# Forgetting attention: queries turned by VectorE in 32x32 blocks instead of by TensorE, and the order of the work around it

## The chip, the core and the metric

The kernel runs on one core of a Trainium2 chip. The metric is the device time of one execution in microseconds (us). Each engine has an instruction queue of its own, worked off in order; engines wait for each other only by counting semaphores. The short names of the profile are used below: PE is TensorE (PEld its weight loads), DVE is VectorE, ACT is ScalarE, POOL is GpSimd, SP issues the weight DMAs.

## The reference, cut to what matters

Two transformer blocks are computed for 256 tokens of width 1024, in fp32. The change is in the first block, which has three mixers side by side (memory cross attention, gated linear attention, forgetting attention). The forgetting attention, with 4 heads of width 128, is:

```python
def _fox(q, k, v, log_f):
    scale = hd ** -0.5
    cum = jnp.cumsum(log_f, axis=-1)
    ...
        logits = (jnp.einsum('bhqd,bhkd->bhqk', q_i, k) * scale
                  + c_i[..., None] - cum[:, :, None, :])
        p = jax.nn.softmax(jnp.where(mask, logits, -jnp.inf), axis=-1)
        return jnp.einsum('bhqk,bhkd->bhqd', p.astype(v.dtype), v)

o_fox = _fox(_rmsnorm(_heads(fq, 4), g_fox_q), _rmsnorm(_heads(fk, 4), g_fox_k), _heads(fv, 4), log_f)
gates = jax.nn.sigmoid(bg + b_gate)      # merged = sum over mixers of gates * (y_b @ w_branch[b])
```

The gains `g_fox_q` and `g_fox_k` belong to the 128 columns of a head, so the product q.k only sees their product, column by column.

## The kernel before, in words

**Weights.** All weights come as 186 granules, nearly all of 128 x 2048 fp32 (1 MB), through a ring of four slots. Per granule, ACT makes the high part (`Wh`, line 1273), DVE the low part (`Wl = raw - Wh`, line 1810), and PE multiplies three times (high x high, low x high, high x low; line 689). A granule is 24 matmuls of 512 columns, 12 for each of the two tiles of 128 tokens. ACT may write a slot of `Wh` when PE has done the granule four earlier (`gran_used`); DVE follows ACT (`hi_ready`); PE and the next DMA follow DVE (`lo_ready`).

**The order of the work** is written by hand, engine by engine. A weight unit is 512 output columns; on ACT and DVE `unit(name, read_out, *urgent)` splits the first granule of the unit four places on, then does the given steps, then splits the last one. The units around the change stand in this order on PE: fq, fk, fv, gate_mem0, gate_gla0, gate_fox0, branch_mem0, branch_gla0, branch_fox0, gate_mem1. A gate unit has two granules, a branch unit one. Each unit's product lies in two of four PSUM banks `ps`, so a unit may start only when the unit two places earlier has been read out of its banks (`drained`). For the gate units DVE takes the product out (line 2027), ACT works on it in the same bank (abs, exp, ln; lines 1480 to 1482), and DVE takes that out (line 2037). For branch_mem0 DVE multiplies out of the bank into `merged` (line 2049).

**The small work** goes through four other PSUM banks `aux0` to `aux3`; `plan_aux` lists which use has which bank, and a use may start when the one before it was read (`aux_free`). Transposes of rows (tokens on partitions) to columns (`turn_rows`, line 761) are PE matmuls with an identity: four blocks of 128x128 for one bank. Then ACT or DVE copy the bank to SBUF. In the forgetting attention: POOL norms the rows `FQ` and `FK`; PE turns `FQ` into banks 0 and 1 and `FK` into banks 2 and 3; ACT copies the first two to `fqT` with the query gain (line 1497), DVE the other two to `fkT` with the key gain (line 1901). One unit later PE makes the scores (`fsc`, lines 1014 and 1015), head h in bank h. DVE adds the forget terms and takes the maximum (lines 2085 to 2093), ACT makes exponentials (line 1452), DVE norms them (`normed`, line 2011), PE turns them (`fpT`, line 761), ACT and DVE copy them, and PE attends (`foT`, line 977). ACT and DVE make high and low parts of the result, `yTh_fox` and `yTl_fox` (line 1829), the operands of branch_fox0.

**What stands around it.** The memory attention's result `moT` takes bank h for head h just ahead of the turns of `FQ` and `FK`; its low parts `yTl_mem` (line 1829) free these banks. The gated linear attention's result `GG` is turned into banks 0 and 1 (`gyT`) between the two granules of gate_gla0; ACT makes `yTh_gla` (line 1304) and DVE `yTl_gla` (line 1834), which frees these two banks for the scores of heads 0 and 1. On ACT and DVE the splits of the second granule of gate_fox0 and of branch_mem0 stand ahead of these two.

Of the kernel before, what the change touches and what calls it, by code (L numbers as in the profile page):

```python
# [22 lines left out]
ALU = mybir.AluOpType  # L23
ACT = mybir.ActivationFunctionType
AX = mybir.AxisListType

P = 128
TOK = 256
# [9 lines left out]
HD = 128  # L38
# [98 lines left out]
def plan_aux():  # L137

    plan, used = {}, [0] * 4

    def use(name, banks, first=0):
        for b, bank in enumerate(banks):
            used[bank] += 1
            plan[(name, first + b)] = (bank, used[bank])

    use("memT", [0, 1, 2, 3])
    use("xT", [0, 1, 2, 3])
    use("small", [0])
    use("rows20", [1])
    use("gaT", [1])  # L150
    use("z", [0])
    use("mkT", [2, 3])
    use("foxcum", [1])
    use("cum", [2])
    use("suf", [3])
    use("dec", [0])
    use("mqT", [1, 2])
    use("foxT", [0])
    use("gqT", [3])
    use("gkT", [0])  # L160
    use("attn", [1, 2])
    use("cs", [3, 0])
    use("o", [1, 2])
    use("msc", [0, 1, 2, 3])
    use("mpT", [0, 1, 2, 3])
    use("moT", [0, 1, 2, 3])
    use("fqT", [0, 1])
    use("fkT", [2, 3])
    use("gyT", [0, 1])
    use("fsc", [0, 1, 2, 3])  # L170
    use("fpT", [0, 1, 2, 3])
    use("foT", [0, 1, 2, 3])
    use("mgT", [0, 1, 2, 3])
    use("x1T", [0, 1, 2, 3])
    use("ffT10", [0])
    use("x2T", [0, 1, 2, 3])
    use("rsc", [0, 1, 2, 3])
    for h in range(4):
        use(f"ro{h}", [2 * h % 4, 2 * h % 4 + 1])
    for h in range(4):  # L180
        use(f"ryT{h}", [2 * h % 4, 2 * h % 4 + 1])
    use("x3T", [0, 1, 2, 3])
    use("x4T", [0, 1, 2, 3])
    use("bqT0", [0, 1])
    use("bkT0", [2, 3])
    use("bsc", [0, 1, 2, 3])
    use("bqT1", [0, 1])
    use("bkT1", [2, 3])
    use("bpT", [0, 1, 2, 3])
    use("bsc", [0, 1, 2, 3], 4)  # L190
    use("boT", [0, 1, 2, 3])
    use("bpT", [0, 1, 2, 3], 4)
    use("boT", [0, 1, 2, 3], 4)
    use("x5T", [0, 1, 2, 3])
    return plan
# [89 lines left out]
def build(nc, wstream, x_in, mem_in, cpack, gpack, wsmall, w_a2, b_a, b_fox, b_gate, post, rett, mobat, dmask, out):  # L285
    ctx = ExitStack()
    with ctx:
# [4 lines left out]
        def at(name, shape, kb, dt=F32):  # L292
            return nc.alloc_sbuf_tensor_at(name, shape, dt, offset=BASE + int(kb * KB))
# [11 lines left out]
        R = 131  # L305
# [12 lines left out]
        FQ = at("FQ", [P, 2, C], R + 24)  # L318
# [15 lines left out]
        mqT = at("mqT", [P, 4, TOK], R + 52)  # L334
        mkT = at("mkT", [P, 4, TOK], R + 56)
        fpT = at("fpT", [P, 4, 2, TOK], R + 52)
        fqT = at("fqT", [P, 4, TOK], R + 60)
        fkT = at("fkT", [P, 4, TOK], R + 64)
        mpT = at("mpT", [P, 4, 2, TOK], R + 60)
        gqT = at("gqT", [P, 2, TOK], R + 60)  # L340
# [2 lines left out]
        prob = at("prob", [P, 4, 2, TOK], R + 68)  # L343
# [63 lines left out]
        def gcol(name, k=0):  # L407
            o, _ = GAIN_COLS[name]
            return gains[:, o + k:o + k + 1]

        def S(name, a=0, b=None):
            o, w = SCAL[name]
            return sc[:, o + a:o + (w if b is None else b)]
# [16 lines left out]
        def sem(name):  # L430
            if name not in sems:
                sems[name] = ctx.enter_context(nc.semaphore(name))
            return sems[name]
# [43 lines left out]
        def wait_aux(eng, name, b=0):  # L477
            k, n = AUX[(name, b)]
            eng.wait_ge(aux_ready[k], n)
            return aux[k]  # L480
# [6 lines left out]
        def free(ins, name, b=0):  # L487

            return ins.then_inc(aux_free[AUX[(name, b)][0]], 1)
# [191 lines left out]
        def _(pe):  # L681
# [82 lines left out]
            def turn_rows(name, rows, b):  # L764

                turn(name, b, [(kk * TOK + t * P, rows[:, t, (2 * b + kk) * P:(2 * b + kk + 1) * P])
                               for kk in range(2) for t in range(2)])
# [21 lines left out]
            def wait_operand(name, banks):  # L789

                for b in banks:
                    wait_read(pe, name, b)
# [55 lines left out]
            o = open_aux("rows20")  # L848
# [14 lines left out]
            o = open_aux("z")  # L863
# [17 lines left out]
            for name, mat in (("cum", "chunk_upto"), ("suf", "chunk_after")):  # L881
                o = open_aux(name)
# [3 lines left out]
            o = open_aux("dec")  # L886
# [34 lines left out]
            for b, chunks in enumerate(((0, 2), (1,))):  # L921
                o = open_aux("cs", b)
# [69 lines left out]
            for h in range(4):  # L992
                wait_read(pe, "mpT", h)
                attend("moT", h, lambda ks: MV[:, ks, h * HD:(h + 1) * HD], mpT)
            pe.wait_ge(sem("fq_unit"), 1)
            for b in range(2):
                turn_rows("fqT", FQ, b)
            pe.wait_ge(sem("fk_unit"), 1)
            for b in range(2):
                turn_rows("fkT", FK, b)  # L1000
# [6 lines left out]
            product("gate_gla0", (xTh, xTl), before={1: turn_gla})  # L1007

            wait_operand("fqT", range(2))  # L1010
            wait_operand("fkT", range(2))
            for h in range(4):
                o = open_aux("fsc", h)
# [231 lines left out]
        def _(act):  # L1245
# [29 lines left out]
            def unit(name, read_out=None, *urgent):  # L1275

                for g in range(G[name], GEND[name] - 1):
                    split(g + RING)
                if read_out:  # L1280
                    read_out()
                for step in urgent:
                    step()
                split(GEND[name] - 1 + RING)
# [188 lines left out]
            def gate_log(b, n, tiles=(0, 1)):  # L1473
                def go():

                    k = 3 * n + BRANCHES.index(b)
                    for t in tiles:
                        o = bank(f"gate_{b}{n}", t)
                        act.wait_ge(sem("gate_z"), 2 * k + t + 1)
                        link(nc.scalar.activation(o, gate[b][:, t, :], ACT.Abs))  # L1480
                        link(nc.scalar.activation(o, o, ACT.Exp, scale=-1.0))
                        nc.scalar.activation(o, o, ACT.Ln, bias=1.0).then_inc(sem("gate_log"), 1)
                return go
# [6 lines left out]
                for h in range(4):  # L1490
                    high("moT", h, yT["mem"][0], (h,))

            def fq_turned():
                act.wait_ge(sem("q_gains"), 2)
                for b in range(2):
                    o = wait_aux(act, "fqT", b)
                    free(nc.scalar.activation(fqT[:, 2 * b:2 * b + 2, :], o[:, :], ACT.Copy, scale=S("gfq_s")), "fqT", b)

            def mem_probs():
                for h in (0, 2):  # L1500
                    probs_T("mpT", h, mpT)

            unit("gate_mem0", mem_probs, mem_high, gate_log("mem", 0), fq_turned)

            def gla_high():
                for b in range(2):
# [290 lines left out]
        def _(dve):  # L1797
# [15 lines left out]
            def unit(name, read_out=None, *urgent):  # L1813
                for g in range(G[name], GEND[name] - 1):
                    split(g + RING)
                if read_out:
                    read_out()
                for step in urgent:
                    step()
                split(GEND[name] - 1 + RING)  # L1820
# [75 lines left out]
            def turned(name, b, dst, scale=None):  # L1896
                o = wait_aux(dve, name, b)
                if scale is None:
                    free(nc.vector.tensor_copy(dst, o[:, :]), name, b)
                else:  # L1900
                    free(nc.vector.tensor_scalar(dst, o[:, :], scale, None, ALU.mult), name, b)
# [25 lines left out]
                low("xT", b, xTl, xTh, (2 * b, 2 * b + 1), "g_mix")  # L1927
            split(3)
            nc.vector.tensor_scalar(S("gmq_s"), gcol("g_mq"), float(HD) ** -0.5, None, ALU.mult).then_inc(sem("q_gains"), 1)
            nc.vector.tensor_scalar(S("gfq_s"), gcol("g_fq"), float(HD) ** -0.5, None, ALU.mult).then_inc(sem("q_gains"), 1)  # L1930
            x_stats("x0")
            unit("mk")
            head_sums("mk")
# [72 lines left out]
            def normed(k, h, pr, rec, total, widths):  # L2006

                link(nc.vector.reciprocal(rec(0, 2), total(0, 2)))
                for t in range(2):
                    v = pr[:, h % 4, t, 0:widths[t]]  # L2010
                    nc.vector.tensor_scalar(v, v, rec(t, t + 1), None, ALU.mult).then_inc(sem(f"{k}_prob"), 1)  # L2011
# [3 lines left out]
                normed("m", h, prob, lambda a, b: S("ms_rec", 2 * h + a, 2 * h + b),  # L2015
                       lambda a, b: S("ms_sum", 2 * h + a, 2 * h + b), (TOK, TOK))
            head_sums("fk")
            unit("fv")

            def gate_rows(b, n):  # L2020

# [12 lines left out]
            def gate_lsig(b, n, t):  # L2034

                dve.wait_ge(sem("gate_log"), 2 * (3 * n + BRANCHES.index(b)) + t + 1)
                nc.vector.scalar_tensor_tensor(out=gate[b][:, t, :], in0=gate[b][:, t, :], scalar=0.0,
                                               in1=bank(f"gate_{b}{n}", t), op0=ALU.min,
                                               op1=ALU.subtract).then_inc(drained["dve"], 1)
# [21 lines left out]
                for h in range(4):  # L2061
                    low("moT", h, yT["mem"][1], yT["mem"][0], (h,))

            def fk_turned():
                for b in range(2):
                    turned("fkT", b, fkT[:, 2 * b:2 * b + 2, :], gcol("g_fk"))

            def mem_probs():
                for h in (1, 3):
                    turned("mpT", h, mpT[:, h, :, :])  # L2070
                gate_rows("mem", 0)()

            unit("gate_mem0", mem_probs, mem_low, lambda: gate_lsig("mem", 0, 0), lambda: gate_lsig("mem", 0, 1), fk_turned)

            def gla_low():
                for b in range(2):
# [16 lines left out]
                    nc.vector.tensor_reduce(S("fs_nm", 2 * h + 1, 2 * h + 2), prob[:, h, 1, :], AX.X, ALU.max, negate=True)\  # L2093
                        .then_inc(sem("f_max"), 1)

            unit("gate_gla0", gla_low, fox_scores)
            for h in range(4):
                dve.wait_ge(sem("f_exp"), 2 * h + 2)
                normed("f", h, prob, lambda a, b: S("fs_rec", 2 * h + a, 2 * h + b),
                       lambda a, b: S("fs_sum", 2 * h + a, 2 * h + b), (P, TOK))  # L2100
            def fox_probs():
                for h in (1, 3):
                    o = wait_aux(dve, "fpT", h)
# [436 lines left out]
```

## Time and profile before

| | |
|---|---|
| median of 3 runs | 1113.65 us (1113.42 to 1113.72) |
| the profiled execution's own time | 1113.15 us |
| its span in the profile | 1111.4 us |
| granted TensorE clock | 1.00 of full speed |
| PE busy | 1102.1 us, 99% of the span |
| DVE, ACT, POOL busy | 70%, 57%, 14% |
| the changed stretch | about 132 to 190 us of the span |

Times in the rows are from the start of the span. In a timeline row stand the start, the length from the first start to the last end, engine, line, operation, output<-input, sizes and count; an idle time ahead of it and who ended it stand in square brackets. Consecutive instructions of an engine overlap by a little, so starts are further apart than the idle time alone would say, and closer than the durations.

### The profile page before, as it was taken

The page shows a single profiled execution, that of the slowest core. Times are in us where ns is not written, and L with a number is a line of the kernel's source. Part 1 is how long each engine was busy: PE and PEld are TensorE (multiplying, and loading weights), DVE is VectorE, ACT ScalarE, POOL GpSimd, SP SyncE. Part 2 cuts the span into 40 slices and gives each one's busy share as a digit, 9 for nine tenths or more (in the row PEclk, how much of TensorE's full clock was granted, in tenths as well). Part 3 has the DMA queues.
Part 4 walks back from the last instruction along what each step waited for, and adds up shares of the span by engine and source line. Part 5 has one row for each costly group of instructions (what it writes and reads, how often), then busy time and mean ns, then how long its engine had stood idle before and what let it go on. Part 6 is the DMA issues. An engine that isn't in the chain of part 4 may idle for free.

```text
span 1111.4 us, 13482 instructions
## 1 busy us (share of the span) xinstructions
PE 1102.1 (99%) x5152; PEld 916.3 (82%) x5152; DVE 781.5 (70%) x858; ACT 636.8 (57%) x788; POOL 153.3 (14%) x111
## 2 busy tenths in 40 slices
PE   8999999999999999999999999999999999999997
PEld 7788888888888888888888888888888888888886
DVE  5745668776568883678448569998465776899942
ACT  6655566655767653654587366554355545656431
POOL 1433700000343410000023000000016100000000
PEclk9999999999999999999999999999999999999999
DMA  9645344645555555555535456546555334545530
GB/s 355 237 169 180 118 185 144 226 171 193 178 197 207 186 185 197 219 208 192 187 114 195 165 184 252 190 156 230 197 186 199 124 139 171 215 173 185 191 145 38
DMA packets 30503, 205.17 MB, mean 185 GB/s; under 512 B 3624, under 2 KB 3792, under 8 KB 6768
## 3 DMA queue, kind: packets, MB, share of 16 engines
q1 hardware_dynamic: 28752, 198.75, 49.4%
q0 software_dynamic: 1696, 5.64, 1.6%
q8 instruction: 39, 0.64, 0.2%
q14 instruction: 16, 0.13, 0.0%
HBM read 203.33 MB, written 1.05 MB: 184 GB/s over the span
## 4 chain that ended last, share of the span: by engine, by line
PE 94%; DVE 3%; ACT 1%; issue 1%; DMA 1%; SPq 0%; DVEq 0%; ACTq 0%
PE ps L689 83%; PE ps L1108 3%; PE aux L761 3%; PE ps L1110 1%; PE ps L811 1%; PE aux L977 1%; PE aux L1145 1%; DMA mrows<-in_mem 1%; ACT Wh L1273 1%; PE aux L1132 0%; DVE sc L2425 0%; DVE Wl L1810 0%; PE aux L963 0%; DVE bprob L2440 0%; DVE prob L2011 0%
## 5 line engine op out<-in xcount | busy, mean ns | idle before, releaser
L689 PE MATMUL ps<-Wh,xT 128*128 128x512 f32 x1792 | 561.3, 391 | 0.0
L1810 DVE TENSOR_TENSOR Wl<-raw,Wh 128x2048 fp32r<-128x2048 f32 x184 | 425.1, 2318 | 181.8 <-ACT Wh L1273 180.9
L1273 ACT ACTIVATE Wh<-raw 128x2048 fp32r<-128x2048 f32 x184 | 350.9, 1914 | 191.2 <-PE ps L689 190.3
L689 PEld LDWEIGHTS ps<-Wh,xT 128*128 128x128 f32 x1792 | 336.5, 188 | 69.9 <-issue 0.7
L689 PE MATMUL ps<-Wl,xT 128*128 128x512 f32 x896 | 348.8, 389 | 0.0
L689 PEld LDWEIGHTS ps<-Wl,xT 128*128 128x128 f32 x896 | 168.3, 188 | 34.3
L689 PE MATMUL ps<-Wh,hTh 128*128 128x512 f32 x256 | 99.8, 390 | 0.0
L689 PE MATMUL ps<-Wh,hTl 128*128 128x512 f32 x256 | 99.7, 389 | 0.0
L689 PE MATMUL ps<-Wl,hTh 128*128 128x512 f32 x256 | 99.7, 389 | 0.0
L2353 DVE STREAM_TRANSPOSE htmp<-held 32x512 f32<-32x512 f32 x128 | 89.9, 703 | 2.7
L641 POOL TENSOR_TENSOR sc<-sc,cst 128x1 f32<-128x1 f32 x8 | 4.5, 558 | 443.0 <-DVE sc L2313 443.0
L689 PEld LDWEIGHTS ps<-Wh,hTh 128*128 128x128 f32 x256 | 48.1, 188 | 10.0
L689 PEld LDWEIGHTS ps<-Wl,hTh 128*128 128x128 f32 x256 | 48.1, 188 | 9.9
L689 PEld LDWEIGHTS ps<-Wh,hTl 128*128 128x128 f32 x256 | 48.1, 188 | 9.9
L1108 PE MATMUL ps<-xT,Wh 128*128 128x512 f32 x128 | 45.3, 399 | 0.0
L525 POOL TENSOR_TENSOR sc<-sc,cst 128x8 f32<-128x8 f32 (+1 forms) x11 | 17.9, 1631 | 166.9 <-DVE sc L1877 146.1
L1698 ACT ACTIVATE held<-ps 128x512 f32<-128x512 f32 x32 | 18.8, 595 | 32.8 <-PE ps L689 32.8
L1110 PE MATMUL ps<-xT,Wl 128*128 128x256 f32 x128 | 36.0, 281 | 0.0
L689 PE MATMUL ps<-Wh,ffTh 128*128 128x512 f32 x88 | 34.4, 391 | 0.0
L689 PE MATMUL ps<-Wh,ffTl 128*128 128x512 f32 x88 | 34.3, 390 | 0.0
L689 PE MATMUL ps<-Wl,ffTh 128*128 128x512 f32 x88 | 34.3, 389 | 0.0
L1317 ACT ACTIVATE xT<-aux,gains 128x128 fp32r<-128x128 f32 x80 | 21.7, 383 | 21.6 <-PE aux L761 21.6
(354 smaller groups left out, 1296.5 us busy)
## 6 DMA issues: line engine op xcount, KB each, us to landing
raw<-in_wstream SPq DMA_DIRECT2D x185, 1024.0 KB, 4.8
grow<-in_post_gains POOLq DMA_DIRECT2D x4, 512.0 KB, 5.6
grow<-in_b_gate POOLq DMA_DIRECT2D x6, 256.0 KB, 3.5
mrows<-in_mem SPq DMA_DIRECT2D x2, 512.0 KB, 5.2
raw<-in_wstream SPq DMA_DIRECT2D x2, 512.0 KB, 6.4
x<-in_x SPq DMA_DIRECT2D x1, 1024.0 KB, 14.6
out<-x SPq DMA_DIRECT2D x4, 256.0 KB, 2.0
rdm<-in_ret_decays POOLq DMA_DIRECT2D x1, 768.0 KB, 5.1
```

Source lines behind the costliest of these rows:

```text
L525: nc.gpsimd.tensor_tensor(S(f"{key}_rstd", 0, n), S(f"{key}_var", 0, n), K("minus_half").broadcast_to([P, n]), ALU.pow).then_inc(sem("norm ...
L689: mm = nc.tensor.matmul(ps[2 * pair + t][:, :], a[:, kt, t * P:(t + 1) * P], w[:, slot, j, :], start=(first and j == 0 and q == 0), stop=( ...
L761: tr = nc.tensor.transpose(o[0:src.shape[1], at:at + P], src, ident)
L811: mm = nc.tensor.matmul(bank("mk", t), a[:, 4 * g + j, t * P:(t + 1) * P], w[:, g, j, :], start=(g == 0 and j == 0 and q == 0), stop=(g == ...
L977: mm = nc.tensor.matmul(o[:, q0:TOK], v(ks), pT[:, h % 4, ks, q0:TOK], start=(ks == 0), stop=(ks == 1))
L1108: nc.tensor.matmul(o[:, :], Wh[:, g % RING, kt % 4, w], xT[:, kt, :, :], start=(kt == 0), stop=False, skip_group_check=True)
L1110: mm = nc.tensor.matmul(o[:, 0:TOK], Wl[:, g % RING, kt % 4, w], xTh[:, kt, :], start=False, stop=(kt == DK - 1), skip_group_check=True)
L1273: nc.scalar.activation(split_view(Wh, g), weight_view(raw, g), ACT.Copy).then_inc(hi_ready, 1)
L1317: nc.scalar.activation(dst[:, k0 + j, t * P:(t + 1) * P], o[:, j * P:(j + 1) * P], ACT.Copy, scale=gcol(gain, k0 + j)).then_inc(sem(f"{nam ...
L1698: nc.scalar.activation(held[:, n // 2, t, n % 2, :], bank(name, t), ACT.Relu).then_inc(drained["act"], 1)
L1810: nc.vector.tensor_tensor(split_view(Wl, g), weight_view(raw, g), split_view(Wh, g).bitcast(F32), ALU.subtract).then_inc(lo_ready, 1)
L2353: i = nc.vector.transpose(dst[b:b + 32, :, :, a:a + 32], src[a:a + 32, :, :, b:b + 32])
```

## The change

1. PE no longer turns `FQ` (8 transposes of 128x128 gone); banks 0 and 1 lose one use. DVE turns it itself, SBUF to SBUF, by 16 transposes of 32x32 blocks, each over both token tiles and four heads (32 partitions x 256 elements). Eight stand inside unit fv, between its two splits, and eight at the end of gate_mem0, ahead of its last split.
2. `fkT` is copied by ACT, without a gain, in place of the two copies of `fqT`. The key gain is multiplied into the query gain `gfq_s`. When DVE has turned the queries (`fq_turned`), ACT scales all of `fqT` in place by it, one instruction of 128x1024. Only then does ACT go on to its next split. PE's scores wait for this (`fq_scaled`).
3. `fqT` lies at another place in SBUF, where `mkT` was.
4. The norming of the forgetting attention's probabilities moves ahead of the last split of gate_gla0 on DVE.

```diff
-    use("fqT", [0, 1])
...
-        fqT = at("fqT", [P, 4, TOK], R + 60)
+        fqT = at("fqT", [P, 4, TOK], R + 56)
...
-            pe.wait_ge(sem("fq_unit"), 1)
-            for b in range(2):
-                turn_rows("fqT", FQ, b)
...
-            wait_operand("fqT", range(2))
+            pe.wait_ge(sem("fq_scaled"), 1)
...
-            def fq_turned():
+            def fox_turned():
+                for b in range(2):
+                    o = wait_aux(act, "fkT", b)
+                    free(nc.scalar.activation(fkT[:, 2 * b:2 * b + 2, :], o[:, :], ACT.Copy), "fkT", b)
                 act.wait_ge(sem("q_gains"), 2)
-                for b in range(2):
-                    o = wait_aux(act, "fqT", b)
-                    free(nc.scalar.activation(fqT[:, 2 * b:2 * b + 2, :], o[:, :], ACT.Copy, scale=S("gfq_s")), "fqT", b)
+                act.wait_ge(sem("fq_turned"), 1)
+                nc.scalar.activation(fqT[:, :, :], fqT[:, :, :], ACT.Copy, scale=S("gfq_s")).then_inc(sem("fq_scaled"), 1)
...
-            nc.vector.tensor_scalar(S("gfq_s"), gcol("g_fq"), float(HD) ** -0.5, None, ALU.mult).then_inc(sem("q_gains"), 1)
+            nc.vector.scalar_tensor_tensor(out=S("gfq_s"), in0=gcol("g_fq"), scalar=float(HD) ** -0.5, in1=gcol("g_fk"),
+                                           op0=ALU.mult, op1=ALU.mult).then_inc(sem("q_gains"), 1)
...
-            unit("fv")
+
+            def turn_heads(key, rows, dst, first, last):
+
+                dve.wait_ge(sem(f"{key}_unit"), 1)
+                src = rows[:, :, :].rearrange("p t (h d) -> p t h d", d=HD)
+                cols = dst[:, :, :].rearrange("p h (t j) -> p t h j", j=P)
+                for ab in range(first, last):
+                    a, b = 32 * (ab // 4), 32 * (ab % 4)
+                    i = nc.vector.transpose(cols[b:b + 32, :, :, a:a + 32], src[a:a + 32, :, :, b:b + 32])
+                if last == 16:
+                    i.then_inc(sem(f"{key}_turned"), 1)
+
+            unit("fv", lambda: turn_heads("fq", FQ, fqT, 0, 8))
...
-            unit("gate_mem0", mem_probs, mem_low, lambda: gate_lsig("mem", 0, 0), lambda: gate_lsig("mem", 0, 1), fk_turned)
+            unit("gate_mem0", mem_probs, mem_low, lambda: gate_lsig("mem", 0, 0), lambda: gate_lsig("mem", 0, 1),
+                 lambda: turn_heads("fq", FQ, fqT, 8, 16))
...
-            unit("gate_gla0", gla_low, fox_scores)
-            for h in range(4):
-                dve.wait_ge(sem("f_exp"), 2 * h + 2)
-                normed("f", h, prob, ...)
+            unit("gate_gla0", gla_low, fox_scores, fox_normed)
```

Where it moves instructions on DVE, at the end of gate_mem0 and the start of gate_gla0. Before:

```order
L1829 TENSOR_TENSOR yTl_mem<-aux,yTh_mem 128x256 x4
L2037 SCALAR_TENSOR_TENSOR gate_mem<-gate_mem,ps 128x512 x2
L1901 TENSOR_SCALAR fkT<-aux,gains 128x512 x2
L1810 TENSOR_TENSOR Wl<-raw,Wh 128x2048 x2
L1834 SCALAR_TENSOR_TENSOR yTl_gla<-aux,gains,yTh_gla 128x256 x4
```

The same place of the changed kernel, whose line numbers differ by a few:

```order
L1827 TENSOR_TENSOR yTl_mem<-aux,yTh_mem 128x256 x4
L2048 SCALAR_TENSOR_TENSOR gate_mem<-gate_mem,ps 128x512 x2
L2025 STREAM_TRANSPOSE fqT<-FQ 32x2x4x32 x8
L1808 TENSOR_TENSOR Wl<-raw,Wh 128x2048 x2
L1832 SCALAR_TENSOR_TENSOR yTl_gla<-aux,gains,yTh_gla 128x256 x4
```

Eight transposes stand where two copies stood, ahead of two splits and of the instructions that free the banks of `gyT`.

On ACT, at the same place. Before:

```order
L1482 ACTIVATE ps<-ps 128x512
L1497 ACTIVATE fqT<-aux,sc 128x512 x2
L1273 ACTIVATE Wh<-raw 128x2048 x2
L1304 ACTIVATE yTh_gla<-aux,gains 128x256 x4
```

And in the changed kernel:

```order
L1478 ACTIVATE ps<-ps 128x512
L1492 ACTIVATE fkT<-aux 128x512 x2
L1495 ACTIVATE fqT<-fqT,sc 128x1024
L1269 ACTIVATE Wh<-raw 128x2048 x2
L1300 ACTIVATE yTh_gla<-aux,gains 128x256 x4
```

One instruction is new, and it waits for DVE's transposes; the two splits stand behind it.

## Rows read from the trace of the kernel before

**Rows 1.** The page's busy time, share of the span and instructions

```profile
PE 1102.1 (99%) x5152; PEld 916.3 (82%) x5152; DVE 781.5 (70%) x858; ACT 636.8 (57%) x788; POOL 153.3 (14%) x111
```

**Rows 2.** Waits of PE's weight loads, whole span: total, times, longest us

```profile
PEld ps L797 <- DVE warm L1914: 1.5, 1, 1.5
PEld aux L761 <- DVE prob L2011: 0.3, 1, 0.3
```

**Rows 3.** The chain of waits in this stretch: start, length, what

```profile
154.42 1.93 ACT Wh L1273
...
175.29 0.55 PE aux L761 x3
```

**Rows 4.** Timeline of PE

```profile
146.92 1.04 PE L761 MATMUL aux<-cst,FQ 128*128 128x128 f32 x8
...
148.58 0.47 PE L689 MATMUL ps<-Wh,xT 128*128 128x512 f32 x1
...
160.49 0.38 PE L1014 MATMUL aux<-fkT,fqT 128*128 128x128 f32 x2
...
161.14 0.38 PE L1014 MATMUL aux<-fkT,fqT 128*128 128x128 f32 x2
...
162.92 0.58 PE L689 MATMUL ps<-Wh,xT 128*128 128x512 f32 x1
...
174.00 1.84 PE L761 MATMUL aux<-cst,prob 128*128 128x128 f32 x12
...
189.23 0.39 PE L689 MATMUL ps<-Wh,yTh_fox 128*128 128x512 f32 x1
```

**Rows 5.** Timeline of DVE

```profile
147.53 0.42 DVE L1829 TENSOR_TENSOR yTl_mem<-aux,yTh_mem 128x256 fp32r<-128x256 f32 x1 [0.44 <-ACT yTh_mem L1300]
...
151.59 1.40 DVE L1901 TENSOR_SCALAR fkT<-aux,gains 128x512 f32<-128x512 f32 x2
153.97 4.70 DVE L1810 TENSOR_TENSOR Wl<-raw,Wh 128x2048 fp32r<-128x2048 f32 x2 [0.97 <-ACT Wh L1273]
158.58 1.66 DVE L1834 SCALAR_TENSOR_TENSOR yTl_gla<-aux,gains,yTh_gla 128x256 fp32r<-128x256 f32 x4
...
170.32 2.28 DVE L1810 TENSOR_TENSOR Wl<-raw,Wh 128x2048 fp32r<-128x2048 f32 x1
...
174.69 0.55 DVE L2011 TENSOR_SCALAR prob<-prob,sc 128x128 f32<-128x128 f32 x2
...
188.14 1.41 DVE L2049 TENSOR_TENSOR merged<-ps,gate_mem 128x512 f32<-128x512 f32 x2
```

**Rows 6.** Waits of DVE between 130 and 149 us

```profile
DVE Wl L1810 <- ACT Wh L1273: 2.0, 1, 2.0
DVE yTl_mem L1829 <- ACT yTh_mem L1300: 1.8, 4, 0.5
DVE gate_mem L2027 <- PE ps L689: 1.1, 1, 1.1
```

**Rows 7.** Timeline of ACT

```profile
152.01 1.93 ACT L1273 ACTIVATE Wh<-raw 128x2048 fp32r<-128x2048 f32 x1
154.42 1.92 ACT L1273 ACTIVATE Wh<-raw 128x2048 fp32r<-128x2048 f32 x1 [0.48 <-PE ps L689]
...
184.47 1.05 ACT L1487 ACTIVATE gate_fox<-gate_fox 128x1024 f32<-128x1024 f32 x1
185.42 1.19 ACT L1300 ACTIVATE yTh_fox<-aux 128x256 fp32r<-128x256 f32 x4
```

**Rows 8.** DVE transposes of 32x256 in the feed-forward stage, timeline

```profile
396.96 3.12 DVE L2154 STREAM_TRANSPOSE ftmp<-fpair 32x256 f32<-32x256 f32 x7
```

**Rows 9.** Timeline of PE at the start of the span

```profile
1.51 3.85 PE L797 MATMUL ps<-warm 128*128 128x512 f32 x9 [1.51 <-DVE warm L1914]
...
6.61 1.64 PE L797 MATMUL ps<-warm 128*128 128x512 f32 x6
9.18 1.09 PE L761 MATMUL aux<-cst,mrows 128*128 128x128 f32 x8 [0.93 <-DMA mrows<-in_mem]
```

More of the change, by code:

```diff
@@ L1501, in mem_probs @@
                     probs_T("mpT", h, mpT)
-            unit("gate_mem0", mem_probs, mem_high, gate_log("mem", 0), fq_turned)
+            unit("gate_mem0", mem_probs, mem_high, gate_log("mem", 0), fox_turned)
             def gla_high():
@@ L2062, in mem_low @@
                     low("moT", h, yT["mem"][1], yT["mem"][0], (h,))
-            def fk_turned():
-                for b in range(2):
-                    turned("fkT", b, fkT[:, 2 * b:2 * b + 2, :], gcol("g_fk"))
             def mem_probs():
@@ L2094, in fox_scores, with fox_normed @@
                         .then_inc(sem("f_max"), 1)
-            unit("gate_gla0", gla_low, fox_scores)
-            for h in range(4):
-                dve.wait_ge(sem("f_exp"), 2 * h + 2)
-                normed("f", h, prob, lambda a, b: S("fs_rec", 2 * h + a, 2 * h + b),
-                       lambda a, b: S("fs_sum", 2 * h + a, 2 * h + b), (P, TOK))
+            def fox_normed():
+                for h in range(4):
+                    dve.wait_ge(sem("f_exp"), 2 * h + 2)
+                    normed("f", h, prob, lambda a, b: S("fs_rec", 2 * h + a, 2 * h + b),
+                           lambda a, b: S("fs_sum", 2 * h + a, 2 * h + b), (P, TOK))
+            unit("gate_gla0", gla_low, fox_scores, fox_normed)
             def fox_probs():
```

## The prediction, made before the changed kernel was run

> **What bounds the kernel now.** I read the page's busy times first: PE works 1102.1 of 1111.4 us, the others have room [rows 1]. So work taken from PE is worth its time, and work given to another engine costs nothing as long as PE never waits for it. PE's waits come next: after the start there is one of 0.3 us for the norming of probabilities at DVE [rows 2]. The chain of waits says how near PE is to more of them: from 154.42 us on it leaves PE, runs through ACT's and DVE's splits and comes back to PE at 175.29, at the turn of these probabilities [rows 3]. In this stretch DVE and ACT have no time to give away. The timelines then give the distance between PE and each thing it waits for. One measure is used throughout: DVE's norming ended at 174.69 + 0.55 = 175.24 [rows 5] and PE went on at 175.29, so PE starts 0.05 us after its releaser.
>
> **What goes from PE, and what is late next.** Turning FQ and FK took PE from 146.92 to 148.58, 1.66 us for 16 transposes (0.104 each) [rows 4]. The eight of FQ are 0.83 us. But those of FK now follow the memory attention at once, and banks 2 and 3 have to be free of it. The low part of head 3 ends at 147.53 + 0.42 = 147.95 [rows 5]; PE starts on bank 3 at 148.00, and four transposes end at 148.42. Before it was 148.58: of 0.83 us, 0.16 is kept.
>
> **The first eight transposes on DVE.** Seven of the same shape took 3.12 us in the feed-forward stage, 0.446 each [rows 8], so eight take 3.57. They stand in unit fv. Behind them DVE waited 2.0 us for ACT, 1.1 for PE and, ahead of the first low part of the memory attention, about 0.5 for ACT [rows 6], 3.6 in all. They fit, to the tenth. If they took longer, the low parts, which wait for ACT by 0.44 each, would catch up to 1.3 us more before PE's turn of FK is late; beyond this PE pays one for one. I take nothing.
>
> **The other eight, and ACT's new instruction.** Here is the cost. They start where the two copies of fkT stood, at 151.59 [rows 5], and end at 155.16. ACT has by then copied fkT (two copies of the size of the old ones, ready before 152.01) and waits; it scales fqT from 155.20. The row of the same size, 128x1024, holds ACT from 184.47 to 185.42, 0.95 us [rows 7]. The first split starts at 156.15, where it was 152.01: 4.14 late. DVE's split follows as ACT's ends, 158.11 for 153.97. ACT's second split runs to 159.9 without a wait (PE has long freed the slot), and DVE's second follows its own first after 2.2 us, at 160.31. Before, it waited for ACT until 154.42 + 1.92 = 156.34 and was over at 158.58, also 2.2 us. So the low parts yTl_gla start at 162.51 instead of 158.58: DVE is 3.93 us late.
>
> Can it catch up? Behind this come the read-out of gate_gla0, ACT's abs, exp and ln, DVE's second read-out, the scores, the norms, two splits, and the same again for gate_fox0. The idle times in it are DVE's waits for ACT's logarithms, which shift along. The order of norms and split changes nothing for what comes behind both. So I carry 3.93 us to the end of this stretch.
>
> **Where PE meets it.** Three places.
> 1. Banks 0 and 1. The scores of heads 0 and 1 need gyT read out by yTl_gla. This ended at 158.58 + 1.66 = 160.24, now at 164.17. PE was at head 1's scores at 161.14 [rows 4], 0.85 behind the release; now it starts them at 164.22, 3.08 late. It stands idle from 160.3 to about 163.4, when bank 0 is free (half of yTl_gla, 0.8 us ahead of its end). gate_fox0 starts at 162.92 + 3.08 = 166.00. That fqT is scaled at 156.2 and fkT copied at 152 is early enough.
> 2. The probabilities. Their norming loses the 2.2 us of the split ahead of it and is 3.93 late: 175.24 + 3.93 - 2.2 = 176.97. PE comes to them at 174.00 + 3.08 = 177.08. No wait, and the 0.3 us of before is gone.
> 3. branch_fox0 follows. PE would be at it at 189.23 + 3.08 - 0.3 = 192.01. Its bank has to be read out of branch_mem0, by DVE's line 2049: the first of two takes half of 1.41 us from 188.14 [rows 5], now from 192.07 to 192.77. PE starts at 192.82, 3.59 late. The low parts yTl_fox end just ahead of this instruction and ask for less.
>
> After branch_fox0 the read-outs lie further ahead of PE, and PE is the bound again. Nothing else is added: one 128x1 instruction differs at the start, the new address of fqT was free since the memory scores, and POOL has FK normed long before PE turns it, also if it shares SBUF with DVE's first transposes.
>
> **Sum.** 0.83 removed from PE and 0.3 of wait, against idle times of about 0.7 (FK's banks), 3.1 (gyT) and 0.8 (branch_mem0's bank), with small change: +3.6 us. The profiled execution took 1113.15 us, so 1116.75; the median stood 0.5 above it, so 1117.2 us on the scale of the medians. What can move the sum by itself is DVE's price per transpose, since eight stand on the path: by 10% either way it is 0.4 us. The ACT instruction is taken from rows of the same size; if it reads and writes one place at another speed, it may be 0.3 off either way. Its own range is 1116.4 to 1118.0.
>
> **Rivals.**
> - *The clock falls in the gap.* PE idles 3.1 us in one piece. The trace has no such gap: 0.93 us at 8.3 us did no harm [rows 9], and after the start's idle the first nine matmuls took 3.85 us, 0.43 each, where six later took 1.64; in the long run one takes 0.23. That is 1.2 GHz against 2.4. If the same comes back after the gap, nine matmuls cost 9 x 0.2 = 1.8 us more. PE would reach branch_fox0 at 193.8, past the bank's 192.82: +4.6 us, 1118.2. For it: the length of the gap. Against it: 150 us of dense work ahead and dense work behind. The Trainium skill (TensorE: Matmul & The Clock Gate, section HAM oscillation) speaks for it: a wait between groups of matmuls can bring the array back to its lower clock. By that rule the time is this rival's; by the trace's one gap inside the work it is not, and that gap is shorter by three times.
> - *DVE's lateness does not reach PE (the other side).* The place is again the end of gate_mem0. PE's delay is DVE's lateness less 0.34, and this is 8 transposes plus 0.36. It comes under 2.23 us (0.2%) if a transpose costs 0.28 or less, or if DVE catches up 1.4 us between 160 and 188. At most PE keeps 0.16 + 0.3 and the time is 1113.2; halfway it is 1115. For it: DVE is busy 70% over the span. Against it: the shape's row says 0.446, and the chain passes through this stretch without a gap.
> - *The gyT wait alone counts*: had line 2049 more room than the rows say, the delay would be 3.08 - 0.3 = 2.8, 1116.4. This lies at the edge of my own range.
> - *Faster by more than 0.2%*: all that PE can gain is 0.83 + 0.3 = 1.1 us. No mechanism reaches 2.2.
>
> **Chances.** The forecast with its edge case 0.74, the clock 0.10, the other side 0.14, anything else 0.02. A measurement of this kernel tells about 0.2% (2.2 us) from no change. The range takes the forecast's own, most of the clock case and the upper part of the other side: 1115.5 to 1118.5. Slower 0.85, the same 0.13, faster 0.02.
>
> **What would show it.** Right: PE idle about 3 us ahead of head 0's scores, released by yTl_gla; another 0.8 ahead of branch_fox0, released by the product of branch_mem0; no wait at the probabilities; ACT idle 3 us ahead of the scaling of fqT; transposes of 0.44 us; FK's turn split by a wait of some 0.4 us between its banks. Wrong: transposes much below 0.4; yTl_gla starting before 161; the granted clock below 1.00 behind the gap; a wait in fv or gate_mem0 that PE has because of the first eight.

## The result, and the profile after

Five executions of the changed kernel took 1119.67 us in the median (1118.91 to 1120.92), those of the kernel before on the same chip 1113.65 (1113.29 to 1114.75): a ratio of 1.0052, 95% interval 1.0038 to 1.0066. It is 6.0 us slower. The forecast was 3.6 us, 1117.2; the time lies above the range. The profiled execution was the shortest of the five, 1118.91 us with a span of 1117.1.

The page's line of busy times, as in [rows 1]: busy us, share of the span, instructions.

```profile
PE 1102.4 (99%) x5144; PEld 914.9 (82%) x5144; DVE 787.1 (70%) x872; ACT 637.9 (57%) x789; POOL 153.2 (14%) x111
```

PE has 8 instructions fewer, DVE 14 more (16 transposes for two copies), ACT one more. That eight transposes less don't show in PE's busy time is in part the start: its first nine matmuls took 4.21 us in this execution for 3.85 [rows 9].

PE's waits between 130 and 200 us: who waited for whom, total us, times, longest. Before, this view was empty for the same stretch; its 0.3 us at the probabilities stood with the weight loads [rows 2].

```profile
PE aux L1010 <- DVE yTl_gla L1832: 3.3, 1, 3.3
PE ps L688 <- DVE merged L2060: 0.7, 1, 0.7
PE aux L760 <- DVE yTl_mem L1827: 0.2, 1, 0.2
```

The three waits that the prediction named are there with their releasers: gyT's banks, branch_mem0's bank, and FK's banks. The last has a second part, between the two banks, which stands with the weight loads (the same view for PEld, 140 to 200 us):

```profile
PEld aux L760 <- DVE yTl_mem L1827: 0.4, 1, 0.4
```

The timeline of PE, for [rows 4]: start, length, what, and in brackets the idle time ahead of it. In this execution all work from 12 us on stands 0.63 us later already, as it began later (the clock rose at 5.91 us and not at 4.82, and the memory rows came later); 0.63 is to be taken off each start to compare it with before.

```profile
147.87 1.43 PE L760 MATMUL aux<-cst,FK 128*128 128x128 f32 x8 [0.16 <-DVE yTl_mem L1827]
...
164.44 0.46 PE L1010 MATMUL aux<-fkT,fqT 128*128 128x128 f32 x2 [3.33 <-DVE yTl_gla L1832]
...
167.01 0.58 PE L688 MATMUL ps<-Wh,xT 128*128 128x512 f32 x1
...
178.14 1.47 PE L760 MATMUL aux<-cst,prob 128*128 128x128 f32 x12
...
193.82 0.47 PE L688 MATMUL ps<-Wh,yTh_fox 128*128 128x512 f32 x1 [0.66 <-DVE merged L2060]
```

So the scores of head 0 stand at 163.81 for 160.49, gate_fox0 at 166.38 for 162.92 (3.46 late), the turn of the probabilities at 177.51 for 174.00 and without a wait, branch_fox0 at 193.19 for 189.23 (3.96 late).

The timeline of DVE, for [rows 5], and of the first eight transposes:

```profile
134.83 3.57 DVE L2025 STREAM_TRANSPOSE fqT<-FQ 32x256 f32<-32x256 f32 x8
138.42 4.50 DVE L1808 TENSOR_TENSOR Wl<-raw,Wh 128x2048 fp32r<-128x2048 f32 x2
...
152.33 3.59 DVE L2025 STREAM_TRANSPOSE fqT<-FQ 32x256 f32<-32x256 f32 x8
159.01 4.49 DVE L1808 TENSOR_TENSOR Wl<-raw,Wh 128x2048 fp32r<-128x2048 f32 x2 [3.08 <-ACT Wh L1269]
163.42 1.66 DVE L1832 SCALAR_TENSOR_TENSOR yTl_gla<-aux,gains,yTh_gla 128x256 fp32r<-128x256 f32 x4
...
192.99 1.41 DVE L2060 TENSOR_TENSOR merged<-ps,gate_mem 128x512 f32<-128x512 f32 x2
```

And of ACT, for [rows 7]:

```profile
156.02 1.15 ACT L1495 ACTIVATE fqT<-fqT,sc 128x1024 f32<-128x1024 f32 x1 [3.44 <-DVE fqT L2025]
157.08 3.70 ACT L1269 ACTIVATE Wh<-raw 128x2048 fp32r<-128x2048 f32 x2
```

This is the chain of the forecast: DVE's transposes, ACT idle 3.44 us until they are done, one instruction, two splits, DVE behind them. yTl_gla starts at 162.79 for 158.58, where 162.51 was forecast.

What the forecast does not have is at the end. DMAs in the last 8 us of the changed kernel: the queue of instructions with packets, MB and share, and the issues of the result with KB each and the median us to landing.

```profile
q14 instruction: 1, 0.01, 0.5%
...
out<-x SPq DMA_DIRECT2D x2, 256.0 KB, 2.5
```

The same view of the kernel before, which has no line of q14:

```profile
out<-x SPq DMA_DIRECT2D x2, 256.0 KB, 2.0
```

And SP's wait for that result, first the kernel after, then before:

```profile
SPq L286 <- DMA out<-x: 2.7, 1, 2.7
```

```profile
SPq L287 <- DMA out<-x: 1.7, 1, 1.7
```

A packet of instructions (8 KB, at 1115.4 us) is fetched while the result is being written, and the kernel sees its result landed 1.0 us later. The kernel before has 16 such packets on this queue and the last came at 978.7 us; the changed kernel has 16 up to 983.3 us and this one more. By the times of the single packets the fetch runs for 0.60 us from 1115.38, and the last 2 KB of the result start at 1115.98, when it is over. It is the same in e2 and e4 below with a fetch of 0.31 us, and in e1 the last 4 bytes of the write start behind it. How the 1.0 us comes from this was not taken apart. From the last instruction of DVE to the end of the span it is 3.47 us, before 2.44.

So the 5.76 us between the two spans (1117.13 and 1111.37) are 0.63 in the first 12 us, 4.06 between 130 and 195 us, 0.04 over the 900 us behind it, and 1.03 at the end. Two terms were not in the forecast, one was a little short, and the medians are still further apart than this shortest execution.

### The profile page after: what moved, and what is told of

Its sections match the earlier page's. It is cut to its first block, busy times and chain, and to the rows that moved or that the text cites. A ratio compares the mean times of both kernels' runs of the same rounds, so it can differ in the third digit from the quotient of the medians.

```text
span 1117.1 us, 13480 instructions
## 1 busy us (share of the span) xinstructions
PE 1102.4 (99%) x5144; PEld 914.9 (82%) x5144; DVE 787.1 (70%) x872; ACT 637.9 (57%) x789; POOL 153.2 (14%) x111
## 3 DMA queue, kind: packets, MB, share of 16 engines
HBM read 203.33 MB, written 1.05 MB: 183 GB/s over the span
## 4 chain that ended last, share of the span: by engine, by line
PE 92%; DVE 4%; ACT 2%; issue 1%; DMA 1%; SPq 0%; DVEq 0%; ACTq 0%
PE ps L688 81%; PE ps L1104 3%; PE aux L760 2%; PE ps L1106 1%; PE ps L810 1%; DVE Wl L1808 1%; PE aux L1141 1%; ACT Wh L1269 1%; DMA mrows<-in_mem 1%; PE aux L976 1%; PE aux L1128 0%; DVE sc L2436 0%; ACT ps L1477 0%; DVE fqT L2025 0%; PE aux L962 0%
```

## The experiments

Three questions were tried: is the stretch's loss made by the chain of transposes, ACT's instruction and splits (**theory A**; the rival is that something shared, such as POOL's work beside DVE's transposes or the new address, slows the stretch); is the end's loss made by the number of DVE's instructions, whatever they do (**theory B**); and what makes the executions of the changed kernel spread over 2 us (**theory C**: the clock falls in PE's gap). Each run stands against the kernel before on its own chip, at 1113.38 to 1113.53 us, and was executed 5 to 11 times.

**e1, the changed kernel once more.** No edit.

> The changed kernel itself, once more. Theory A (mechanism alone): the compute ends about 4.1 us later than before, as in the first trace (PE waits of 3.3 us at head 0's scores and 0.7 at branch_fox0), and this is in every run. The first trace has two more parts, 0.6 us in the first 12 us of the span and 1.0 us behind the last DVE instruction, where DMA queue 14 fetches 8 KB at 1115.4. Theory B: both come with the program and return here, total +5.7 to +6.3 us. Theory C: one or both are luck of one execution; then the total is +4.1 to +5.1 us and the trace shows the gap behind the last DVE instruction at 2.4 us, not 3.5.

Measured: 1119.44 us (1118.06 to 1121.54), ratio 1.0056 [1.0043, 1.007]. The first real matmul stands at 10.55 us, so the 0.6 us at the start belonged to one execution. The end's 3.60 us came again. And this execution has the clock's fall. Busy times and granted clock of stretches around PE's gap (from:to, us, busy of PE, PEld, DVE, ACT, POOL, then the clock, share of DMA, GB/s):

```profile
150.00:160.00 10.00, 10.00 (x50) 8.36 (x49) 5.80 (x10) 6.53 (x7) 0.60 (x1) 1.00 0.09 26
160.00:163.80 3.80, 0.48 (x3) 0.08 (x2) 3.80 (x5) 2.54 (x6) 0.00 (x0) 1.00 0.43 155
163.80:167.60 3.80, 3.79 (x13) 3.26 (x14) 2.56 (x5) 2.37 (x5) 0.00 (x0) 0.55 0.99 375
167.60:175.00 7.40, 7.40 (x35) 6.16 (x34) 6.18 (x21) 6.20 (x17) 0.54 (x1) 1.00 0.16 50
```

PE worked without a break, sat idle for 3.3 us, went on, and then the granted clock was half (1.2 of 2.4 GHz) from 164.13 us for 3.4 us. The scores were made meanwhile:

```profile
163.81 0.47 PE L1010 MATMUL aux<-fkT,fqT 128*128 128x128 f32 x2 [3.32 <-DVE yTl_gla L1832]
164.10 1.03 PE L1011 MATMUL aux<-fkT,fqT 128*128 128x256 f32 x2
...
167.99 0.58 PE L688 MATMUL ps<-Wh,xT 128*128 128x512 f32 x1
```

From head 0's scores to gate_fox0 it is 4.18 us, in the first profile of this kernel 2.57. Of these 1.6 us, 0.8 are left behind branch_fox0, since PE no longer waits there for branch_mem0's bank: that was 0.7 us.

**e2, the kernel before with 14 more instructions on DVE.**

```diff
             nc.vector.memset(warm[:, :].bitcast(F32), 1.0).then_inc(sem("warm_rows"), 1)
+            for k in range(14):
+                nc.vector.memset(S("spare", k, k + 1), 0.0)
```

> The kernel before with 14 memsets of 128x1 on DVE at its start, where DVE waits for a DMA: the changed kernel has 14 DVE instructions more (872 for 858). 
Measured: 1114.55 us against 1113.38, ratio 1.0011 [1.0002, 1.002]. The end takes 3.49 us, and the same line of the DMA view as in the changed kernel has appeared:

```profile
q14 instruction: 1, 0.01, 0.2%
...
out<-x SPq DMA_DIRECT2D x2, 256.0 KB, 2.5
```

Fourteen instructions of no weight, 1100 us away from the end, cost 1.2 us. By the traces 1.05 of it is at the end (3.49 for 2.44). Theory B stands.

**e3, the changed kernel with 40 more**, so that DVE's program has crossed that border earlier. The edit is e2's with 40 for 14.

> The changed kernel with 40 such memsets on DVE at its start. Theory B: the page is crossed 40 instructions earlier, under other work, so the end gets its 2.4 us back: 1.0 us faster than the changed kernel, about +4.7 us on the kernel before, with a fetch of queue 14 some tens of us ahead of the end. Theory C: the same as the changed kernel.

Measured: 1118.03 us (1117.24 to 1119.16), ratio 1.0041 [1.0027, 1.0055]. The last packet of instructions now comes at 1034.3 us, the end takes 2.44 us, and the median is 1.4 us below e1's although the kernel does more. The executions of the two overlap (e1's start at 1118.06), so the size is better taken from the traces: 1.0 us. All profiles agree: with 872 instructions on DVE (the changed kernel, e1, e2, e4) the last packet comes behind DVE's last instruction, with 858 (the kernel before, e5) at 978 to 979 us, with 906 or 912 (all others) at 1030 to 1036 us.

**e4, the gain in the copy of the keys**: ACT's instruction on `fqT` and PE's wait for it are gone, the chain loses this link alone.

```diff
-            pe.wait_ge(sem("fq_scaled"), 1)
+            pe.wait_ge(sem("fq_turned"), 1)
...
-                    free(nc.scalar.activation(fkT[:, 2 * b:2 * b + 2, :], o[:, :], ACT.Copy), "fkT", b)
-                act.wait_ge(sem("q_gains"), 2)
-                act.wait_ge(sem("fq_turned"), 1)
-                nc.scalar.activation(fqT[:, :, :], fqT[:, :, :], ACT.Copy, scale=S("gfq_s")).then_inc(sem("fq_scaled"), 1)
+                    free(nc.scalar.activation(fkT[:, 2 * b:2 * b + 2, :], o[:, :], ACT.Copy, scale=S("gfq_s")), "fkT", b)
```

> The changed kernel, but ACT multiplies both gains into fkT as it copies it, and the instruction that scales fqT is gone: ACT no longer waits for DVE's transposes, PE waits for these alone. Theory A: of DVE's lateness of 4.2 us at yTl_gla (3.93 by the forecast's sum), about 3 came from ACT standing still behind the transposes. Now DVE's split starts at 155.2 on the clock of before instead of 153.97, yTl_gla is 1.0 us late, the scores' wait falls to under 0.5 us and branch_fox0 is 0.7 us late; with the end's 1.0 us and the start's 0.6 the total is +0.7 to +2.3 us. Rival: DVE's transposes alone are to blame (3.6 us added to DVE), and the wait stays above 2 us, total above +4 us.

Measured: 1115.55 us, ratio 1.0018 [1.0009, 1.0027]. PE's waits in the stretch, as above:

```profile
PE ps L688 <- DVE merged L2058: 0.7, 1, 0.7
PE aux L1010 <- DVE yTl_gla L1830: 0.3, 1, 0.3
PE aux L760 <- DVE yTl_mem L1825: 0.2, 1, 0.2
```

The wait of 3.3 us is 0.3. ACT splits while DVE transposes, and the low parts are 1.15 us late instead of 4.2 (159.91 less 0.18 for this execution's start, against 158.58). The end is still 3.48 us, 1.0 of the 2.2 us that this kernel loses. branch_fox0 is 0.89 us late for 3.96. Theory A stands: all sixteen transposes are still there beside the same work of POOL and at the same address, and nine tenths of the wait are gone.

**e5, the order of the norms alone**, on the kernel before.

```diff
-            unit("gate_gla0", gla_low, fox_scores)
-            for h in range(4):
...
+            def fox_normed():
+                for h in range(4):
...
+            unit("gate_gla0", gla_low, fox_scores, fox_normed)
```

> The kernel before with the fourth part of the change alone: probabilities normed ahead of the last split of gate_gla0. Theory: it takes away PE's one wait of 0.3 us at 175.3 and changes nothing behind both: -0.3 us, no wait at the turn of the probabilities, branch_fox0 0.3 us earlier. Rival: it hides a larger gain or loss (the split comes 2.6 us later and branch_gla0 or the read-outs wait for it): anything beyond 0.5 us.

Measured: 1113.33 us against 1113.53, ratio 0.9998 [0.9989, 1.0007]. In the profile branch_fox0 starts 0.23 us earlier, less than a comparison of times can tell. PE waits for nothing in the stretch.

**e6, the kernel before with eight unneeded transposes** at the end of gate_mem0, written to a free place that nobody reads, and 40 more small instructions as in e3, so that the end is not disturbed.

```diff
-            unit("gate_mem0", mem_probs, mem_low, ..., fk_turned)
+            unit("gate_mem0", mem_probs, mem_low, ...,
+                 lambda: turn_heads("fq", FQ, spareT, 8, 16), fk_turned)
```

> The kernel before, and on DVE at the end of gate_mem0 eight transposes of FQ that nobody needs, written to free space; PE still turns FQ, ACT does not wait for DVE. 40 memsets at DVE's start keep the page crossing away from the end. Theory: fkT's copies start at 155.2 for 151.6, the split at 156.6 for 153.97, yTl_gla 2.4 us late; PE 1.5 us late at head 1's scores and, without the moved norms, 2.4 us at the turn of the probabilities: +2.4 us. That is what DVE's part costs alone. Rival (contention or latencies beyond the queue's order): over 3 us.

Measured: 1115.97 us against 1113.53, +2.44, ratio 1.0021 [1.0012, 1.0031]. The low parts of the gated attention are 2.48 us late, of 3.6 us of transposes: the 0.97 that DVE waited for ACT [rows 5] take up most of the difference. Eight transposes alone, with no ACT behind them, cost three fifths of the stretch's loss. They cost more than in e4, since here DVE also keeps its two copies of fkT (1.40 us), which are ACT's in e4. PE meets the lateness at two places, first at yTl_gla and then, as the norms are not moved here, at the probabilities (a wait of its weight loads):

```profile
PE aux L1015 <- DVE yTl_gla L1835: 1.4, 1, 1.4
PEld aux L762 <- DVE prob L2014: 1.3, 4, 0.3
```

**e7, e4 with the second eight transposes spread**: two ahead of each of DVE's two waits for ACT's logarithms, four behind; and the 40 of e3.

```diff
-            unit("gate_mem0", mem_probs, mem_low, lambda: gate_lsig("mem", 0, 0), lambda: gate_lsig("mem", 0, 1),
-                 lambda: turn_heads("fq", FQ, fqT, 8, 16))
+            unit("gate_mem0", mem_probs, mem_low, lambda: turn_heads("fq", FQ, fqT, 8, 10), lambda: gate_lsig("mem", 0, 0),
+                 lambda: turn_heads("fq", FQ, fqT, 10, 12), lambda: gate_lsig("mem", 0, 1), lambda: turn_heads("fq", FQ, fqT, 12, 16))
```

> The kernel with the gain in the key copy, and four of the second eight transposes put where DVE waits for ACT's logarithms in gate_mem0 (two ahead of each of the two read-outs); 40 memsets at DVE's start. Theory: four are left on the path, 1.8 us for the 1.4 of fkT's copies and 1.0 of idle time: yTl_gla is on time, PE waits nowhere at the scores, keeps 0.16 + 0.3 us and meets branch_mem0's bank 0.36 us earlier than before: -0.3 to -0.4 us. Rival: DVE's lateness was not what PE waited for: then the time stays at +1 us, as with the gain in the key copy without the fetch at the end.

Measured: 1113.2 us against 1113.53, ratio 0.9999 [0.999, 1.0008]. PE's wait for FK's banks is still there (0.2 us, and 0.4 at the weight loads), and nothing else holds it in the stretch; branch_fox0 starts at 188.83, 0.40 earlier than before. With its queries turned by DVE the kernel is 6 us faster than the changed kernel, of which 1.0 are owed to the 40 small instructions, and level with the one before: what it wins on that, 0.3 us, is less than can be measured.

**e8, e7 with two more steps moved**: PE turns `GG` ahead of `FK`, and DVE reads branch_mem0 out ahead of the last split of gate_fox0.

```diff
+            pe.wait_ge(sem("go_unit"), 1)
+            for b in range(2):
+                turn_rows("gyT", GG, b)
             pe.wait_ge(sem("fk_unit"), 1)
...
-            product("gate_gla0", (xTh, xTl), before={1: turn_gla})
+            product("gate_gla0", (xTh, xTl))
...
-            unit("gate_fox0", fox_probs, gate_rows("fox", 0))
+            unit("gate_fox0", fox_probs, gate_rows("fox", 0), branch_rows("mem", 0))
...
-            unit("branch_mem0", branch_rows("mem", 0))
+            unit("branch_mem0")
```

> As the one before, and gyT is turned ahead of fkT (banks 0 and 1 are free there, so PE does not wait for banks 2 and 3), and DVE reads branch_mem0 out ahead of the last split of gate_fox0, where it waits for ACT. Theory: PE keeps all 0.83 us and the 0.3; yTl_fox becomes the nearest, ending 0.7 us ahead of where PE was: -0.7 us on the kernel before, 1.5 to 1.8 us of gain against the kernel with the gain in the key copy and without the fetch. Rival: nothing is left to gain (-0.3 us as the one before).

Measured: 1113.2 us against 1113.53, ratio 0.9999 [0.999, 1.0008]: the gain of 0.7 us that was expected did not come, the rival's 0.3 did. PE is 0.74 us early at the probabilities, and gives back 0.3 at branch_fox0:

```profile
PE ps L688 <- DVE yTl_fox L1823: 0.5, 1, 0.5
```

With the bank read out early, branch_fox0's operands end last.

**e9, the gap filled, and e10, the gap open.** Both are the kernel of e3. In e9 PE makes 12 unneeded matmuls ahead of its wait for the scores' operands, into a bank that gate_fox0 overwrites.

```diff
+            pe.wait_ge(lo_ready, G["gate_fox0"] + 1)
+            wait_drained(pe, "gate_mem0", 0)
+            for _ in range(12):
+                nc.tensor.matmul(bank("gate_fox0", 0), xTh[:, 0, 0:P], Wh[:, G["gate_fox0"] % RING, 0, :], start=True, stop=True)
             pe.wait_ge(sem("fq_scaled"), 1)
```

> The changed kernel with 40 one-element memsets ahead on VectorE (so that no fetch of instructions falls into the last microseconds), and with 12 unneeded 512-column matmuls on TensorE in front of its wait for the first use of the scaled fox queries, written into a bank that the next matmul that matters overwrites from the start: TensorE now idles for about 0.7 us less than the 3.3 us there (12 x 0.22 us = 2.6 us at the full clock). What it waits for is not touched. Theory C (some executions of the changed kernel lose 0.8 us because the clock falls to half behind the 3.3 us in which TensorE idles): the idle time is 0.7 us or less, the clock stays at 1.0 there, the slowest of the executions come down by about 0.8 us, and the median lies 0.3 to 0.8 us under that of the same kernel with the gap open (e10), at about 1117.3; the stretch up to branch_fox0 takes the same time in the profile. Rival (the spread of the changed kernel has another cause, the start for instance): median and spread as with the gap open, within 0.2 us, or 0.1 to 0.3 us longer since the fill delays the first matmul behind it.

> The kernel of e3 once more, as the pair of e9 on the same chip: the changed kernel with 40 one-element memsets ahead on VectorE, the gap in front of the scaled queries left open. All theories: about 1118.0, as before (1117.2 to 1119.2). Theory C: spread of 1.5 us or more between its executions, the longer ones with the clock at half for about 3.4 us behind the gap; if the profiled execution is one of those, the stretch from the first use of the scaled queries to branch_fox0 takes 30.1 us in it, else 29.4 us. Rival: the stretch takes 29.4 us in a long execution too.

Measured: e9 1117.47 us (1117.39 to 1117.5), e10 1117.94 (1117.62 to 1118.32), before 1113.44; ratios 1.0036 [1.0023, 1.005] and 1.004 [1.0026, 1.0053]. The intervals of the ratios overlap, yet all five executions of e9 lie within 0.11 us and below all five of e10. PE's gap of e9 in the timeline:

```profile
160.46 2.88 PE L1009 MATMUL ps<-Wh,xT 128*128 128x512 f32 x12
163.95 0.46 PE L1014 MATMUL aux<-fkT,fqT 128*128 128x128 f32 x2 [0.60 <-DVE yTl_gla L1836]
```

Granted clock of e9 and then of e10, in the 4 us behind the gap, columns as in e1:

```profile
164.00:168.00 4.00, 4.00 (x22) 3.44 (x23) 2.59 (x5) 2.63 (x5) 0.00 (x0) 1.00 0.90 369
```

```profile
164.00:168.00 4.00, 3.90 (x15) 3.37 (x16) 2.74 (x5) 2.48 (x5) 0.00 (x0) 0.63 0.91 375
```

The profiled execution of e10 is its longest, 1118.32 us: half a clock from 165.03 us for 3.4 us, and 30.22 us from head 0's scores to branch_fox0. That of e9 took 1117.49, with the clock at full speed and 29.39 us. Theory C stands: PE was busy with work that nobody needs, and the kernel ran faster. The Trainium skill (TensorE: Matmul & The Clock Gate, section HAM oscillation) says that a wait between groups of matmuls can bring the array back to its lower clock; the traces of e1 and e10 agree, with 3.3 us idle and 3.4 us at 0.5. Those of the changed kernel's first profile and of e3 do not: they have the same 3.3 us gap and the clock at 1.00 behind it.

The mean granted clock of the executions that were not profiled says how often it happens. The two profiled executions with the fall have 0.997, the two without it 0.999 and 1.000. Of the 20 executions with the 3.3 us gap, 13 are at 0.997 or below: 4 of 5 of the changed kernel, 4 of 5 in e1, 3 of 5 in e3, 2 of 5 in e10. Of the 132 other executions of the experiments, those of the kernel before and of e9 included, one is (0.948). In e10 the two at 1.000 took 1117.62 us, the three at 0.997 and 0.998 took 1117.94 to 1118.32.

## Why the prediction was wrong

**The mechanism was right, step by step.** Times of after have the start's 0.63 taken off.

| step | forecast | measured |
|---|---|---|
| first eight transposes | hidden, yTl_mem on time | 3.57 us, hidden; last part of yTl_mem at 147.53, as before |
| FK's turn, wait between banks | about 0.4 | 0.4, and 0.2 ahead of the turn; gate_gla0 0.16 early (forecast 0.16) |
| ACT scales fqT, holds ACT for | 0.95 us | 1.06 (156.02 to 157.08) |
| start of yTl_gla | 162.51 | 162.79 |
| PE's idle time ahead of the scores | 3.1 | 3.3 |
| wait at the probabilities | none | none |
| start of branch_fox0 | +3.59 | +3.96, later units +4.06 |

**The stretch's term was 0.4 to 0.5 us short.** The transposes cost what the row of the feed-forward stage said (3.59 for 3.57). The low parts were 0.28 us later than forecast: 0.11 is ACT's instruction, which was named as uncertain by 0.3, and 0.11 lies ahead of the transposes, which start at 151.70 for 151.59. The rest is the change of engine: from the last transpose to ACT it takes 0.10 us and not the 0.04 that I put there. For ACT's 0.11 the prediction's reason, reading and writing one place, does not hold: the row that it took the price from, gate_fox<-gate_fox, does so too. What differs is the gain that ACT reads for each partition (`sc` in the row). A copy of 128x512 took 0.69 us with it (fqT before, fkT in e4) and 0.60 without it (fkT after). The remaining 0.1 lies between the read-out of branch_mem0 and PE. With this term alone the time is 1117.2 + 0.47 = 1117.7, inside the range; e9, which has this term and neither of the two below, measured +4.03 us and 1117.47.

**The step that failed is "Nothing else is added".** I looked there for costs of the removed and new instructions where they stand. The number of DVE's instructions has a cost of its own at another place: 858 became 872, and with them came one more packet of instructions, in the last two microseconds, where it lies beside the write of the result. It is 1.03 us by the traces and 1.2 by the times of e2. Added to the 1117.7 it gives 1118.7 to 1118.9, above the range by itself. No rival held it. The trace of before gives the places of its 16 packets, and I did not look.

**The clock's rival was given too little.** I put the clock and the forecast side by side as if one of them were to happen in all executions, at 0.10 for the clock, and took nothing of it into the sum. By the mean clocks it happens in 13 of 20, in 4 of 5 of the measured executions of the changed kernel. Where it does, the rival's sizes hold: nine matmuls' worth of 1.8 us was 1.6, and branch_fox0 at 193.8 was 193.97 in e1. My reason against it (dense work on both sides) is refuted: behind 150 us of dense work the clock fell. To the median it adds 0.5 us in e10 (less e9), where it came in two or three of five executions. A single execution with it loses 0.8 (30.22 for 29.39 us), so where four of five have it, the median can hold up to that.

**The sum again**: 4.0 for the stretch (e9), 1.0 to 1.2 for the end (traces, e2), 0.5 to 0.8 for the clock: 5.5 to 6.0 of the measured 6.0. Nothing further is needed for the median, though a rest of up to 0.5 us would not show among executions that spread over 2 us. The other side's rival fell: it wanted transposes of 0.28 us or a DVE that catches up, and DVE gave nothing back over 30 us, as its idle times are waits for ACT.

What stays open is what decides whether the clock falls in an execution, and why the longest ones (1120.92 us of the changed kernel, 1120.38 and 1121.54 in e1) lose 1.4 to 2.5 us more than e1's profiled one: none of them was profiled.

## What to carry to other kernels

Where PE is busy 99% of the span, a cheap instruction that makes ACT wait for DVE costs what is queued behind it: here 1 us of scaling put the whole 3.6 us of transposes ahead of two splits, and moving the gain to the operand that was ready anyway took it out. Before a change that adds instructions, look in the trace at when the last packets of instructions come; a few more instructions can bring one more packet beside the last write, and then two versions should be compared with this taken out of both, as in e3. And price an idle time of TensorE of some microseconds with the clock that may be lost behind it, as a term that need not come in every execution.

## What the runs showed of the hardware

- In these traces instructions come on two queues of their own: q14 with 16 or 17 packets of 8 KB and q8 with 39 of 16 KB. One packet of q14 in the last microseconds made the kernel see its result landed 1.0 us later, 2.7 for 1.7 us; fourteen DVE instructions of 128x1 at the start of the kernel decided over it (e2).
- After 3.3 us idle the granted clock was 0.5 for 3.4 us in two of four profiled executions that had this gap (the mean clocks say 13 of all 20), and it fell 0.3 to 0.9 us after PE had taken up its work, not in the gap itself. With 0.6 us idle in its place (e9) it stayed at 1.00.
- An ACT copy of 128x512 fp32 from PSUM took 0.09 us longer with a scale read per partition (0.69 us, before and e4) than without (0.60, after).
- A DVE transpose of 32x256 fp32 took 0.45 us beside POOL's work (134.83, first eight) as without it (152.33, second eight).
